# A hybrid attention layer: the second row tile of the first attention transposed by VectorE in 32x32 blocks and placed by DMAs, with its value products six steps later

## The reference, cut to what matters

```
h = x @ w_in                                   # all projections at once
A: DSA attention, 8 heads of 64: a small indexer picks the 128 keys of each query;
   p = softmax(q k^T * scale, only picked and causal keys);  o_a = (p @ v) * silu(gate_a)
B: latent attention, 8 heads (64 + 32 rotary), causal:
   p = softmax(q k^T * scale);                               o_b = (p @ v) * silu(gate_b)
out = concat(o_a, o_b) @ w_out
y = LayerNorm(2**0.25 * x + out)
```

## Time and profile before

| | us |
|---|---|
| median of three runs | 281.82 (281.43 to 281.95) |
| the profiled execution: its own time | 281.9 |
| its span in the profile | 280.1 |
| TensorE busy | 271.5 (97%) |
| VectorE busy | 232.5 (83%) |
| GpSimd busy | 188.2 (67%) |
| ScalarE busy | 150.1 (54%) |

### The profile page before, as it was taken

How to read it: one execution, slowest core, us unless ns; L and a number is a source line. 1 busy time by engine, 2 the same in 40 slices (tenths; PEclk the granted TensorE clock), 3 DMA queues, 4 the chain that set the end, 5 groups by cost and what they waited for, 6 DMA issues and landing times.

```text
span 280.1 us, 5091 instructions
## 1 busy us (share of the span) xinstructions
PE 271.5 (97%) x1640; PEld 226.6 (81%) x1640; DVE 232.5 (83%) x528; ACT 150.1 (54%) x352; POOL 188.2 (67%) x209
## 2 busy tenths in 40 slices
PE   8999999999999999999999999999999999999990
PEld 7999987778888888888888888887668788888890
DVE  1899998999999999999985598777695795886675
ACT  4656544675443377215168697786677785432000
POOL 5998999844099999999945995694699940300012
PEclk9999999999999999999999999999999999999996
DMA  7986554222614297221218861916730036252412
GB/s 232 362 265 161 152 145 136 84 77 65 159 15 138 75 228 220 80 75 40 75 41 224 250 161 19 243 46 219 265 121 0 2 108 195 69 157 77 150 75 75
DMA packets 21641, 36.97 MB, mean 132 GB/s; under 512 B 7184, under 2 KB 9744, under 8 KB 21360
## 3 DMA queue, kind: packets, MB, share of 16 engines
q1 hardware_dynamic: 20752, 35.77, 43.5%
q10 hardware_dynamic: 864, 0.88, 1.2%
HBM read 26.69 MB, written 2.10 MB: 103 GB/s over the span
## 4 chain that ended last, share of the span: by engine, by line
PE 90%; DVE 2%; DMA 2%; SPq 2%; ACT 1%; issue 1%; DVEq 0%
PE ps L1343 51%; PE ps L1661 12%; PE ps L1583 5%; PE ps L1544 5%; PE ps L1602 3%; PE ps L1623 3%; PE ps L1526 2%; PE ps L1359 2%; SPq L434 2%; PE ps L1529 2%; PE ps L1453 2%; DMA w_raw<-in_w_in 1%; PE ps L1563 1%; DMA turn_pT<-turn_st 1%; DVE turn_st L1220 1%; PE ps L1634 1%
## 5 line engine op out<-in xcount | busy, mean ns | idle before, releaser
L642 POOL TENSOR_TENSOR w_lo<-w_raw,w_hi 128x512 fp32r<-128x512 f32 (+3 forms) x62 | 84.6, 1388 | 16.9 <-ACT w_hi L787 16.2
L787 ACT ACTIVATE w_hi<-w_raw 128x512 fp32r<-128x512 f32 (+3 forms) x62 | 35.9, 594 | 55.9 <-PE ps L1343 52.0
L1661 PE MATMUL ps<-wo_hi,oT 128*128 128x512 f32 (+1 forms) x144 | 45.4, 388 | 0.0
L898 ACT ACTIVATE probs<-probs,small 128x512 f32<-128x512 f32 (+3 forms) x64 | 35.6, 557 | 14.6 <-DVE small L1170 13.4
L1343 PE MATMUL ps<-w_hi,x_lo 128*128 128x512 f32 (+3 forms) x120 | 42.9, 361 | 0.0
L1343 PE MATMUL ps<-w_lo,x_hi 128*128 128x512 f32 (+3 forms) x120 | 42.9, 361 | 0.0
L1343 PE MATMUL ps<-x_hi,w_hi 128*128 128x512 f32 x96 | 38.0, 396 | 0.0
L1343 PE MATMUL ps<-x_hi,w_lo 128*128 128x512 f32 x96 | 37.4, 390 | 0.0
L1343 PE MATMUL ps<-x_lo,w_hi 128*128 128x512 f32 x96 | 37.4, 390 | 0.0
L1343 PE MATMUL ps<-w_hi,x_hi 128*128 128x512 f32 (+2 forms) x84 | 32.1, 382 | 0.0
L1661 PEld LDWEIGHTS ps<-wo_hi,oT 128*128 128x128 f32 x144 | 25.7, 189 | 5.0 <-issue 0.2
(11 more groups left out here) (200 smaller groups left out, 627.9 us busy)
## 6 DMA issues: line engine op xcount, KB each, us to landing
w_raw<-in_w_in SPq DMA_DIRECT2D x20, 512.0 KB, 3.7
kaT_swap<-kaT SPq DMA_DIRECT2D x8, 256.0 KB, 3.8
w_raw<-in_w_out SPq DMA_DIRECT2D x4, 512.0 KB, 4.9
wo_early<-in_w_out SPq DMA_DIRECT2D x4, 512.0 KB, 5.9
wo_raw_b<-in_w_out SPq DMA_DIRECT2D x4, 512.0 KB, 5.2
x_res<-in_x SPq DMA_DIRECT2D x4, 512.0 KB, 3.6
x_raw<-in_xT SPq DMA_DIRECT2D x3, 512.0 KB, 6.3
qT_turned<-qT SPq DMA_DIRECT2D x4, 256.0 KB, 4.1
```

The costliest lines, as they stand in the source:

```text
L642: pool.tensor_tensor(w_lo[:, s, 0:n], w_raw[:, s, 0:n], w_hi[:, s, 0:n], ALU.subtract).then_inc(w_lo_ready, 1)
L787: act.activation(dst, w_raw[:, s, 0:n], ACT.Copy).then_inc(w_hi_ready, 1)
L898: act.activation(probs[:, u % NPROBS, 0:N], probs[:, u % NPROBS, 0:N], ACT.Exp, bias=neg_max[:, u % 8:u % 8 + 1], scale=-1.0, accum_out=ro ...
L1661: ins = mm(out_ps(i, b), oT[i % 2][:, o, k, :], w[:, wcols], start=first, stop=final)
```

## The change

Four things change together.

1. The 8 units of v = 1 (even units 16 to 30) are no longer transposed by TensorE and no longer copied by VectorE. VectorE turns each in 32x32 blocks by two instructions (`turn_a`), from `probs` into two staging tiles `a_turn_st`, at the place where the copy stood (step u + 3). The first of them waits for the 16 value products of units 0 to 15, since a staging tile overlaps their transposed copies. The mask of unit u + 4 now waits for the turn of unit u.
2. After the last turn SyncE issues 16 DMAs of 96 KB that place the blocks in `a_turn_pT`. `load_rows(0)` moves behind them and behind A's last value product.
3. The value products of v = 1 are left out of the bursts of steps 28 and 36 and are done at step 42 (`outputs_turned`), when all 16 DMAs have landed. VectorE's first turn of B (step 43) waits for them.
4. The gate of v = 2 is now turned and applied before that of v = 1 (`TURN_RANK`, `TURN_AT`, `GATE_AT`), and the two halves of the output sums swap banks in `ps_y`, so that the first half (step 40) needs v = 2 only and the second (step 44) needs v = 1, gated in VectorE's step 43.

Places of the remaining transposed copies change with it (`PLACES`), and those placed at 94 KiB and above wait for `qpe_placed`.

```diff
-    TURN_RANK = [0, 1, 2, 3]
+    TURN_RANK = [0, 2, 1, 3]
+    A_TURNED = 1
...
         a, b = place_of(u)
-        return max([w for w in range(u) if place_of(w)[0] < b and a < place_of(w)[1]], default=None)
+        return max([w for w in range(u) if not a_blocks(w) and place_of(w)[0] < b and a < place_of(w)[1]], default=None)
...
+    def a_blocks(u):
+
+        return unit(u)[0] == A_TURNED
+
+    def a_block_count(u):
+        return sum(a_blocks(w) for w in range(u + 1))
...
-        if not by_blocks(u):
+        if not by_blocks(u) and not a_blocks(u):
             slots.append(u)
...
+    a_turn_st = [sb(f"a_turn_st{n}", kib, [P, 2, HEADS, ORDER[A_TURNED] + 1, SQ]) for n, kib in enumerate((24, 88))]
+    a_turn_pT = sb("a_turn_pT", 178, [P, 4, HEADS, ORDER[A_TURNED] + 1, SQ])
...
-            bank = (ps_s[:, 0], ps_s[:, 1], ps_o[:, 0])[b] if i == TT - 1 else ps_y[:, b]
+            bank = (ps_s[:, 0], ps_s[:, 1], ps_o[:, 0])[b] if i == TT - 1 else ps_y[:, 1 - b]
...
-            return u < NU_A and u % 2 == 0
+            return u < NU_A and u % 2 == 0 and not a_blocks(u)
...
                 if last_user(u) is not None:
-                    eng.wait_ge(pv_done, HEADS * (last_user(u) // HEADS + 1))
+                    eng.wait_ge(pv_done, pv_count(last_user(u)))
+                if place_of(u)[0] >= 94:
+                    eng.wait_ge(qpe_placed, 16 * P // SQ)
...
+            sp.wait_ge(a_turned, 2 * HEADS)
+            for c in range(4):
+                for a in range(4):
+                    sp.dma_start(a_turn_pT[SQ * c:SQ * (c + 1), a],
+                                 a_turn_st[c // 2][SQ * a:SQ * (a + 1), c % 2]).then_inc(a_placed, 16)
+            sp.wait_ge(pv_done, NU_A)
             load_rows(0)
-            sp.wait_ge(pv_done, NU_A)
             sp.dma_start(lng[:, :], ln_g.broadcast_to([P, D_MODEL])).then_inc(ln_loaded, 16)
...
+                if a_blocks(u - NPROBS):
+                    dve.wait_ge(a_turned, 2 * a_block_count(u - NPROBS))
+                elif by_blocks(u - NPROBS):
                     dve.wait_ge(blocks_turned, block_count(u - NPROBS))
...
+            def turn_a(u):
+                v, m, h, N = unit(u)
+                dve.wait_ge(probs_ready, u + 1)
+                if h == 0:
+                    dve.wait_ge(pv_done, BLOCK_UNITS)
+                src = probs[:, u % NPROBS, 0:N].rearrange("p (j c t) -> p j c t", c=4, t=SQ)
+                for n in range(2):
+                    V.transpose(a_turn_st[n][:, :, h].rearrange("p c j t -> p j c t"), src[:, :, 2 * n:2 * n + 2]).then_inc(a_turned, 1)
...
-                dve.wait_ge(pv_done, BLOCK_UNITS * (A_RANK.index(v) // 2 + 1))
+                dve.wait_ge(pv_done, NU_A if v == A_TURNED else pv_count(BLOCK_UNITS * (A_RANK.index(v) // 2 + 1) - 1))
...
+                if u == HEADS * (TT + 1):
+                    dve.wait_ge(pv_done, NU_A)
...
                 for w in turned_at(u):
                     if by_dve(w):
                         copy_probsT(w)
+                    elif a_blocks(w):
+                        turn_a(w)
...
                 for w in (u - 7, u - 6, u - 3, u - 2):
-                    v, m, h, N = unit(w)
+                    if a_blocks(w):
+                        continue
                     for a in range(2):
                         wait_copied(pe, w + 2 * a)
-                    for j in range(m + 1):
-                        for a in range(2):
-                            ins = mm(oa_bank(v)[A_DIM * a:A_DIM * (a + 1), h // 2 * P:(h // 2 + 1) * P],
-                                     va[:, j, (h + a) * A_DIM:(h + a + 1) * A_DIM],
-                                     probsT[w + 2 * a][:, j * P:(j + 1) * P], start=(j == 0), stop=(j == m))
-                            if j == m:
-                                ins.then_inc(pv_done, 1)
+                    values_a(w, [probsT[w + 2 * a][:, :].rearrange("p (j t) -> p j t", t=P) for a in range(2)])
+
+            def values_a(w, pT):
+                v, m, h, N = unit(w)
+                for j in range(m + 1):
+                    for a in range(2):
+                        ins = mm(oa_bank(v)[A_DIM * a:A_DIM * (a + 1), h // 2 * P:(h // 2 + 1) * P],
+                                 va[:, j, (h + a) * A_DIM:(h + a + 1) * A_DIM], pT[a][:, j], start=(j == 0), stop=(j == m))
+                        if j == m:
+                            ins.then_inc(pv_done, 1)
+
+            def outputs_turned():
+                pe.wait_ge(a_placed, 16 * 16)
+                for w in range(NU_A):
+                    if a_blocks(w) and unit(w)[2] % 2 == 0:
+                        values_a(w, [a_turn_pT[:, :, unit(w)[2] + a].rearrange("p s j t -> p j s t") for a in range(2)])
...
-                            pe.wait_ge(o_ps_read, TURN_RANK.index(A_RANK[2 + b]) + 1)
+                            pe.wait_ge(o_ps_read, TURN_RANK.index(A_RANK[3 - b]) + 1)
...
-                    if not by_blocks(w):
+                    if not by_blocks(w) and not a_blocks(w):
                         transposes(w)
...
+                if u == A_TURNED_AT:
+                    outputs_turned()
...
-GATE_AT = [28, 37, 39, 45]
+TURN_AT = [28, 39, 37, 44]
+GATE_AT = [28, 43, 38, 45]
+A_TURNED_AT = 42
...
-          [(30, 24, 25.5, 27, 28.5), (91, 88, 89, 92, 93)]]
+          [(30, 24, 25.5, 27, 28.5), (30, 31, 201, 205, 94)]]
```

More of the change, by code:

```diff
@@ L114, in place_of @@
         n, r = divmod(u, BLOCK_UNITS)
-        start = PLACES[n][r % 2][r // 2 % 5]
+        start = PLACES[n][r % 2][r // 2 % len(PLACES[n][r % 2])]
         return start, start + unit(u)[3] * 4 / 1024
@@ L223, in build @@
     rope_tmp = sb("rope_tmp", 114, [P, 2, TT, (IDX_HEADS + 1) * IDX_DIM])
-    probsT = [sb(f"probsT{u}", place_of(u)[0], [P, unit(u)[3]]) for u in range(NU_A)]
+    probsT = {u: sb(f"probsT{u}", place_of(u)[0], [P, unit(u)[3]]) for u in range(NU_A) if not a_blocks(u)}
     causal = sb("causal", 194, [P, SEQ])
@@ L305, in build @@
         sums_b_ready, scaled_b, blocks_turned = sem("sums_b_ready"), sem("scaled_b"), sem("blocks_turned")
+        a_turned, a_placed = sem("a_turned"), sem("a_placed")
         blocks_placed = {v: sem(f"blocks_placed{v}") for v in TURNED}
@@ L406, in wait_copied, with pv_count @@
             else:
-                eng.wait_ge(probsT_copied, u + 1 - n - sum(by_blocks(w) for w in range(u + 1)))
+                eng.wait_ge(probsT_copied, u + 1 - n - block_count(u) - a_block_count(u))
+        def pv_count(u):
+            end = HEADS * (u // HEADS + 1)
+            return end - a_block_count(end - 1)
         def copy_free(eng, u):
@@ L950, in _ @@
                 for w in turned_at(u):
-                    if not by_dve(w) and not by_blocks(w):
+                    if not by_dve(w) and not by_blocks(w) and not a_blocks(w):
                         copy_probsT(w)
@@ L1165, in mask_unit @@
                     dve.wait_ge(bias_ready, 1)
-                if by_blocks(u - NPROBS):
+                if a_blocks(u - NPROBS):
+                    dve.wait_ge(a_turned, 2 * a_block_count(u - NPROBS))
+                elif by_blocks(u - NPROBS):
                     dve.wait_ge(blocks_turned, block_count(u - NPROBS))
@@ L1708 @@
 VB_AT = [2, 2, 2, 4, 4, 6, 6, 8, 10, 14, 16, 18]
-TURN_AT = [28, 36, 38, 44]
-GATE_AT = [28, 37, 39, 45]
+TURN_AT = [28, 39, 37, 44]
+GATE_AT = [28, 43, 38, 45]
+A_TURNED_AT = 42
 A_T_LAG, A_PV_LAG = 3, 5
```

## The result

The changed kernel takes 297.55 us (median of 6 runs, 296.92 to 299.65) against 281.82 us: ratio 1.0567, 95% interval 1.0545 to 1.0589. The side was forecast, the size was not: +15.7 us instead of +3.0.

A forecast was written before the change was run, and what follows sets the result against it. VectorE was taken to bound steps 21 to 28, TensorE from step 37, then a chain without room from step 45. Terms 1.25 - 1.40 + 2.84 + 0.3 = +3.0 on 281.9 gave 284.9 us, range 280.8 to 286.9.

The forecast's parts named there:

- the rivals: Own waits free 283.7 us (0.18), TensorE the bound 279.3 (0.22), nearly cancelling 282.7 or 282.0 (0.12), late DMAs 286.4 or 288 (0.10).
- the range's end, 286.9: Upper end of the forecast time in us, with the worst case of late DMAs left out.
- value products of step 42: TensorE, step 42: 24 products (48 records) moved there add 2.84 us where TensorE is the bound.
- step 45: Where the chain passes from TensorE to VectorE: +3.0 us, carried to the end.
- The first wait: VectorE, step 19: the first turn waits for 16 value products and holds later masks; mask 21 +0.85 us.
- the longer turns: VectorE, between masks 21 and 28: a pair of turns 0.80 us against a copy's 0.46, four times, +1.32.
- the gate of step 28: VectorE, step 28: the gate follows mask 28 by about 1.8 us instead of 2.03; mask 29 +0.98.
- The rule of the Trainium skill: VectorE: a semaphore costs nothing extra; as a rival, a pair of turns at 0.59, 283.7 us, chance 0.18.
- the case in which TensorE is the bound: Rival: TensorE's matmuls show no gap, so removed transposes save 2.64 us; 279.3 us, chance 0.22.
- The landing of the placing DMAs: Before step 42: landed at 209.5 to 210.1, TensorE asks at 211.2; no wait, 1.1 to 1.7 us to spare.
- Step 44: TensorE's second half of the output sums waits for the gate of v = 1: +0.3 us.
- Nothing there with room, one to one: From step 45 to the end: no room to absorb a delay, so step 45's delay reaches the end in full.

The follow-up runs named there:

- e2: The kernel before with only the wait for qpe_placed added for places at 94 KiB and above (units 7 and 9); 294.33 us, ratio 1.0424.
- e1: The changed kernel with the wait for qpe_placed kept only for places from 94 to 98 KiB, so units 7 and 9 no longer wait; 286.46 us, ratio 1.0164.
- e5: e3 with the gate of v = 1 moved to the start of VectorE's step 43; 284.91 us, ratio 1.0114; repeated unchanged, 285.02 us.
- e4: The kernel before with part 4 of the change alone (order of the gates, swapped banks); 282.47 us, ratio 1.0009.
- e9: e1 with the 24 value products of step 42 done twice; 287.62 us, ratio 1.0222.
- e3: e1 with units 18 to 30 turned ahead of the step's mask instead of behind it; 285.48 us, ratio 1.0122.
- e6: e2 with 36 extra matmuls at step 12 that keep TensorE at work while it would stand; 291.55 us, ratio 1.0345.
- e8: e5 with ScalarE's share of B's placing DMAs issued one step later (PLACE_AT 52 instead of 51); 285.51 us, ratio 1.0145.
- e10: e5 with TensorE's second burst of value products (units 8 to 15) done in step 19 instead of 20; 283.38 us, ratio 1.0061.

## Why the prediction was wrong, point by point

**The step that failed** is one that the prediction did not take: it put the wait for `qpe_placed` at nothing without a reason, and by itself that wait costs 12.0 us (`e2`) of the 15.7. The change's part on places ("those placed at 94 KiB and above wait for `qpe_placed`") has no term in the sum, though the sum goes through the change part by part. The condition reads like one on the new places of v = 2 (201, 205, 94), whose copies come at 184 us and later, behind the DMAs. But `copy_free` is called for the first block too, and its list of places was not held against 94. Two rows would have shown the price: in the kernel before, the queue of SyncE, and ScalarE's copy of unit 7,

```profile
173.99 3.85 SPq L522 DMA_DIRECT2D qbT<-qpe_blk  x4
...
170.37 0.26 ACT L917 ACTIVATE probsT<-ps 128x128 f32<-128x128 f32 x1
```

which stands there at 170.37 us. The page has 3.9 us from such an issue to its landing, and the fourth starts at 177.2, so the wait ends near 181. None of the rivals had this mechanism, and the range's end, 286.9, was set by the costs that had been looked for.

**All other steps**, read in `e1`, where the wait is gone. Its profiled execution is some 0.6 us ahead of the other already at 15 us, in the first loads (SyncE's long series of 13 loads starts at 14.51 us instead of 15.05), where nothing was changed; the two executions of `e5` differ there too (15.37 and 15.64). So both are set to mask 19 (178.44 here, 179.04 before: add 0.60). VectorE of `e1`:

```profile
178.44 0.36 DVE L1195 CUSTOM_DVE_ANT_0 probs<-ps,score 128x256 f32<-128x256 f32 x1
...
181.72 0.64 DVE L1219 STREAM_TRANSPOSE a_turn_st<-probs 128x192 f32<-128x192 f32 x2 [2.92 <-PE ps L1645]
182.50 0.56 DVE L1195 CUSTOM_DVE_ANT_0 probs<-ps,score 128x384 f32<-128x384 f32 x1
...
182.99 0.42 DVE L1195 CUSTOM_DVE_ANT_0 probs<-ps,score 128x256 f32<-128x256 f32 x1
...
188.92 0.56 DVE L1195 CUSTOM_DVE_ANT_0 probs<-ps,score 128x384 f32<-128x384 f32 x1
...
191.35 0.41 DVE L1195 CUSTOM_DVE_ANT_0 probs<-ps,score 128x256 f32<-128x256 f32 x1
...
192.47 0.56 DVE L1195 CUSTOM_DVE_ANT_0 probs<-ps,score 128x384 f32<-128x384 f32 x1
```

and its chain from step 42 on:

```profile
210.79 2.77 PE ps L1645 x48
213.56 0.86 PE ps L1582 x2
...
215.50 0.59 DVE gate L1234
216.09 0.04 issue
216.13 0.96 PE ps L1709 x3
...
222.01 0.04 DVE probs L1195
...
231.42 1.31 SPq L452
...
235.96 2.70 DMA turn_pT<-turn_st
238.66 0.14 issue
238.80 2.84 PE ps L1671 x48
```

| after minus before, us | forecast | `e1` |
|---|---|---|
| mask 21 | +0.85 | +0.93 |
| mask 28 | +2.17 | +2.18 |
| mask 29 | +0.98 | +1.01 |
| mask 30 | +1.31 | +1.31 |
| value products of step 42 | +2.84 | +2.77 |
| step 43's scores (before: 211.39) | +2.7 | +2.8 |
| step 45 (mask; before 218.99) | +3.0 | +3.6 |
| B's products at step 57 | +3.0 | +4.2 |

The last +4.2 is also the difference of the times (286.46 against 282.26 us on that chip).

- The first wait, the longer turns and the gate of step 28 came out within 0.1 us. The wait for the 16 value products idles VectorE 2.92 us; the turn of a unit costs 0.78 up to the mask that waits for it (181.72 to 182.50; 0.80 forecast). The mask starts 0.14 behind the turn's end, as in the earlier trace rows; unheld, a pair costs 0.56 (`e5`). The rule of the Trainium skill that the prediction weighed (VectorE: DVE Perf Modes, The DRAIN you can't avoid), that a semaphore costs nothing extra, is contradicted here: 0.2 us a pair. The prediction took the overlap of 0.08 us for a second contradiction; it is none, since the same section says that a next instruction that is not held starts earlier.
- TensorE's transposes came off for nothing in steps 21 to 28, as argued; the case in which TensorE is the bound is refuted by `e1`.
- The landing of the placing DMAs was no wait, but nearer than forecast: 16 issues took 11.2 us in `e1` instead of 10.6 at most.
- Step 44 was mis-sized: forecast +0.3, measured about +0.85. The wait itself is as forecast: the first product starts 1.71 us behind the end of step 43's scores (214.42 to 216.13) instead of 1.34, +0.37. But the products behind the wait take 0.96 instead of 0.71, and the scores behind the burst 0.86 instead of 0.66. `e4` has the first two of the three by itself (+0.64); `e5` took 0.6 back.
- "Nothing there with room, one to one" held up to step 50 (`e9`). Then 0.6 us more came in B's placing: 0.3 because SyncE's first nine issues took 6.36 us instead of 6.06 (one took 1.31 us, where none before took more than 0.83), and 0.3 because the last DMA landed after 2.70 us instead of 2.44.
- In the changed kernel itself, from mask 19 to mask 45, 5.2 us were lost instead of the 3.6 of `e1`. Its scores of units 32 to 34 ran while the granted clock was 0.66 over 205 to 210 us (1.70 us for the first, 1.05 in the earlier trace rows). The added wait alone does not bring this second fall: in `e2` the same stretch takes 39.93 us against 39.95 before. Nor is the wait needed for such a fall: `e3` has one (0.67 over 185 to 190 us). No run isolates what sets it off: ahead of it TensorE of `e3` stood 1.11 us behind the first turn, just as in `e1` and `e5`, where the clock stayed at 1.00. The six runs of `e1` spread as well, four at 285.4 to 286.6 and two at 288.2 us; the granted clock of the whole run (0.988 in these two, 0.989 in one of 285.6) does not tell them apart.

## What to carry to other kernels

A condition in a helper that many units share must be evaluated for every caller, not only for those that the change is about: list who newly satisfies it, with the time at which each asks and the time at which the semaphore is reached. A wait put on a copy that empties one of two PSUM banks stops TensorE within two units, and here it then cost some of its clock as well. And work taken off TensorE in a stretch paced by VectorE gives nothing, while work moved into a stretch paced by TensorE is paid in full.

## What the runs showed of the hardware that was not expected

- A stand of 9.2 us of TensorE cost another 2.2 us through the granted clock (`e2` against `e6`); idle time filled with 36 useless matmuls made the kernel faster.
- The clock fell behind short stands too, and not each time. In `e3` TensorE stood 1.11 us (to 183.20), and the clock granted from 185 to 188 us was 0.50; in the changed kernel it stood 0.59 and 0.76 us (to 203.72 and 204.97), and the clock was 0.50 from 206 to 208 us. `e1` and `e5` have the same stand of 1.11 us and kept 1.00. What tells them apart is open.
- A 96 KB placing DMA on SyncE's queue takes 0.59 us to issue, but single ones took 1.3 to 1.7 us. In `e1`, `e3`, `e5` and its repeat, `e8` and `e10` one of them was the fourth of the ten that stand on the path; in the kernel before, in `e2`, `e4`, `e6`, `e9` and in the changed kernel none was. In `e3`, `e5`, its repeat and `e10` one of ScalarE's own issues in the same stretch took 1.2 to 2.0 us as well. The cause is open; `e8` does not exclude the collision of the two queues.
